# State-space tiles: panel splits issued later, gate Silu once per group, skip factor on ScalarE, last group in pieces, stick-breaking mask on GpSimd

## What is computed

```python
def _ssd_chunked(xs, dt, a_neg, bm, cm):        # 4 groups x 8 heads x 64, chunks of 128 tokens
    ...
    def step(state, inp):
        xc, ac, bc, cc = inp
        acum = jnp.cumsum(ac, axis=1)
        seg = jnp.where(causal, acum[:, :, None] - acum[:, None, :], -jnp.inf)
        scores = jnp.einsum('btgn,bsgn->btsg', cc, bc)[..., None] * jnp.exp(seg)
        y_diag = jnp.einsum('btsgh,bsghp->btghp', scores, xc)
        y_off = jnp.einsum('btgn,bghpn->btghp', cc, state) * jnp.exp(acum)[..., None]
        w_end = jnp.exp(acum[:, -1:] - acum)
        new_state = (state * jnp.exp(acum[:, -1])[..., None, None]
                     + jnp.einsum('bsgn,bsghp->bghpn', bc, xc * w_end[..., None]))
        return new_state, y_diag + y_off

# mixer: xbc = silu(conv4(h @ in_w)); after the scan
    y = y + d_skip.astype(jnp.float32)[:, None] * xs.astype(jnp.float32)
    y = y.reshape(b, s, M_D_INNER) * jax.nn.silu(z.astype(jnp.float32))
    yg = y.reshape(b, s, M_GROUPS, M_D_INNER // M_GROUPS)
    yg = yg * lax.rsqrt(jnp.mean(yg * yg, axis=-1, keepdims=True) + EPS)
    y = yg.reshape(b, s, M_D_INNER) * norm_g.astype(jnp.float32)
    return y.astype(h.dtype) @ out_w

# stick-breaking attention, per block of 128 queries
    mask = ((lo + jnp.arange(SB_BLOCK))[:, None] > jnp.arange(hi)[None, :])[None, None]
    log_keep = jnp.where(mask, jax.nn.log_sigmoid(-z), 0.0)
    after = lax.cumsum(log_keep, axis=3, reverse=True) - log_keep
    log_a = jnp.where(mask, jax.nn.log_sigmoid(z) + after, -jnp.inf)
```

## Time and profile before

| | |
|---|---|
| Runs, median (lowest to highest) | 3469.09 us (3468.8 to 3474.67) |
| The profiled execution, own time | 3467.17 us |
| Its span, first to last instruction | 3465.5 us |
| TensorE busy | 3122.3 us (90%) |
| VectorE, ScalarE, GpSimd busy | 1830.7, 1020.5, 421.3 us |
| Mean granted TensorE clock | 0.946 of full speed |

### The profile page before, as it was taken

How to read it: one execution, slowest core, us unless ns; L and a number is a source line. 1 busy time by engine, 2 the same in 40 slices (tenths; PEclk the granted TensorE clock), 3 DMA queues, 4 the chain that set the end, 5 groups by cost and what they waited for, 6 DMA issues and landing times.

```text
span 3465.5 us, 40303 instructions
## 1 busy us (share of the span) xinstructions
PE 3122.3 (90%) x16613; PEld 2420.0 (70%) x16613; DVE 1830.7 (53%) x1822; ACT 1020.5 (29%) x1252; POOL 421.3 (12%) x368
## 2 busy tenths in 40 slices
PE   4988799999979999999978999999966997999987
PEld 3765456666768888888756786878755885666666
DVE  6444683454244454443366756657554226776752
ACT  3111424454121111111123424333232113444432
POOL 0001000000131111110131302021124003000001
PEclk8988899999979999999979999999978999999998
DMA  5333000000114333331113324232310221112201
GB/s 207 109 98 98 28 1 1 1 1 7 43 37 122 109 102 110 121 97 49 38 31 89 104 66 117 67 110 85 91 61 19 85 91 61 43 49 62 74 19 61
DMA packets 241698, 239.28 MB, mean 69 GB/s; under 512 B 11701, under 2 KB 207122, under 8 KB 241554
## 3 DMA queue, kind: packets, MB, share of 16 engines
q1 hardware_dynamic: 219024, 163.34, 15.7%
q0 software_dynamic: 16080, 54.30, 5.0%
q10 hardware_dynamic: 6450, 19.57, 1.6%
HBM read 210.83 MB, written 26.35 MB: 68 GB/s over the span
## 4 chain that ended last, share of the span: by engine, by line
PE 75%; DVE 14%; ACT 5%; issue 3%; POOL 2%; DMA 1%; ACTq 0%; DVEq 0%; POOLq 0%
PE PU L830 14%; PE PU L831 14%; PE PU L832 14%; PE PU L1123 3%; DVE n_h L2131 2%; PE PU L1079 2%; PE PM L1430 2%; PE PM L1418 2%; PE PM L1145 2%; PE PM L1132 2%; PE PU L1407 2%; PE PM L1450 1%; PE PU L844 1%; PE PM L1452 1%; PE PM L1451 1%
## 5 line engine op out<-in xcount | busy, mean ns | idle before, releaser
L830 PE MATMUL PU<-hH,w_hi_t 128*128 128x512 f32 (+1 forms) x1920 | 769.0, 401 | 37.8 <-DVE w_lo_t L2052 31.5
L831 PE MATMUL PU<-hL,w_hi_t 128*128 128x512 f32 (+1 forms) x1920 | 755.4, 393 | 0.0
L832 PE MATMUL PU<-hH,w_lo_t 128*128 128x512 f32 (+1 forms) x1920 | 755.3, 393 | 0.0
L830 PEld LDWEIGHTS PU<-hH,w_hi_t 128*128 128x128 f32 (+1 forms) x1920 | 364.7, 190 | 120.5 <-DVE w_lo_t L2052 34.2
L2052 DVE TENSOR_TENSOR w_lo_t<-w_raw,w_hi_t 128x1024 fp32r<-128x1024 f32 x189 | 244.6, 1295 | 355.3 <-ACT w_hi_t L1508 315.6
L832 PEld LDWEIGHTS PU<-hH,w_lo_t 128*128 128x128 f32 (+1 forms) x1920 | 364.1, 190 | 79.9
L831 PEld LDWEIGHTS PU<-hL,w_hi_t 128*128 128x128 f32 (+1 forms) x1920 | 365.0, 190 | 77.5 <-issue 2.2
L1508 ACT ACTIVATE w_hi_t<-w_raw 128x1024 fp32r<-128x1024 f32 x173 | 180.8, 1045 | 535.2 <-PE PU L832 417.8
L2450 DVE SCALAR_TENSOR_TENSOR xT<-PU,mod,xT 128x1024 f32<-128x1024 f32 x120 | 154.0, 1283 | 207.9 <-PE PU L832 207.9
L844 PE MATMUL PU<-hH,w_hi_t 128*128 128x512 f32 (+1 forms) x272 | 117.2, 431 | 88.2 <-DVE hL L2116 87.8
L2708 DVE TENSOR_TENSOR_SCAN s_keep<-s_keep,zero 128x256 f32<-128x256 f32 (+7 forms) x128 | 184.5, 1442 | 1.8 <-ACT s_keep L1957 1.8
(11 more groups left out here) (358 smaller groups left out, 5171.9 us busy)
## 6 DMA issues: line engine op xcount, KB each, us to landing
ada_w<-in_ada_w_dram POOLq DMA_DIRECT2D x64, 384.0 KB, 4.1
w_raw<-in_w_gu_dram SPq DMA_DIRECT2D x44, 512.0 KB, 3.8
w_raw<-in_m_in_w_dram SPq DMA_DIRECT2D x40, 512.0 KB, 4.1
ada_w<-in_w_ada_dram POOLq DMA_DIRECT2D x32, 512.0 KB, 4.6
seg<-decay_sums SPq DMA_DIRECT2D x32, 512.0 KB, 4.6
w_raw<-in_w_down_dram SPq DMA_DIRECT2D x22, 512.0 KB, 3.6
w_raw<-in_w_in_dram SPq DMA_DIRECT2D x17, 512.0 KB, 3.8
ada_w<-in_w_ada_dram SPq DMA_DIRECT2D x16, 512.0 KB, 18.1
```

The source lines that it names most:

```text
L830: mm(PU[0:width, up, half, :], whi, aH[:, k, cols], start=k == 0, stop=False)
L831: mm(PU[0:width, up, half, :], whi, aL[:, k, cols], start=False, stop=False)
L832: last = mm(PU[0:width, up, half, :], wlo, aH[:, k, cols], start=False, stop=k == kt - 1)
```

## The change

- **Splits**: in the tile part the `split()` of an even tile moves behind `decays` on ScalarE and between `segments` and `masked` on VectorE.
- **Gate**: in groups 0 to 2 the four z units are evacuated with Copy, and after tile 7 ScalarE applies Silu to all four (`z_act`), ahead of the next group's first `split()`. Group 3 keeps Silu at each odd tile.
- **Skip factor**: the GpSimd multiply L769 goes. ScalarE scales the x tile in place, after `token_major`, before the store to `scr_x`. The factor's load and copy move to an earlier place.
- **Group 0**: on VectorE `step_sizes_2` runs before `conv(0, 0)`, and splits run ahead of `step_sizes_3`, `step_sizes_4` and `decay_tables`. On TensorE the scores of tile 0 move into the middle of the first z unit, those of tile 1 behind it.
- **Group 3's end**: tiles 0 to 6 are gated before `output(3, 7)`, tile 7 after it; TensorE sums each of the four squared tiles (32 matmuls for 8) and the GpSimd additions go; scale and low halves alternate, and the first projection unit waits for one tile at a time.
- **Stick-breaking mask**: the two bf16 matmuls of a step go. GpSimd sets the masked part of the last 128 columns of `s_keep` to 1 (two `affine_select` of 128x128 fp32 a step), between ScalarE's sigmoid and VectorE's scan, which now waits for it (`s_mk`). The GpSimd gate multiplies follow at fixed steps.
- Two semaphores of the rotary tables become one.

```diff
@@ -764,10 +761,8 @@
                         g.wait_ge(ss_y, TT * i + c)
                     nc.gpsimd.tensor_tensor(xdt[:, :].rearrange("p (h d) -> p h d", h=8), x3, heads(dt_t, i, c),
                                             ALU.mult).then_inc(ss_x, 1)
-                    g.wait_ge(el_landed[c % 2], 48 * (4 * i + c // 2 + 1))
-                    skip = xl[:, c % 2, :, :]
-                    nc.gpsimd.tensor_tensor(skip, skip, d_col[:, i, :].unsqueeze(2).broadcast_to([P, 4, P]),
-                                            ALU.mult).then_inc(ss_x, 1)
+                if i == NG - 1:
+                    break
                 sq = [xt[:, :, f * P:(f + 1) * P] for f in range(4)]
                 for dst, src, ready in ((sq[0], sq[1], 2), (sq[2], sq[3], 4)):
                     g.wait_ge(m_sq, 4 * i + ready)
...
-                                    base=0, pattern=[[-1, P]], channel_multiplier=1).then_inc(s_mk, 1)
+            link(nc.gpsimd.memset(zero[:, :], 0.0))
             nc.gpsimd.memset(s_keep[:, :, T:T + 1], 1.0).then_inc(s_mk, 1)
-            for n in range(2 * (SB_PAIRS - 1)):
+
+            def next_gate(n):
+
                 g.wait_ge(z_s, n + 1)
                 z = s_z[:, (n // 2 + 1) % 2, n % 2 * 512:(n % 2 + 1) * 512]
                 nc.gpsimd.tensor_tensor(z, z, z_sig[:, :], ALU.mult).then_inc(z_m, 1)
+
+            for s in range(SB_STEPS):
+                for n in (2 * s, 2 * s + 1):
+                    g.wait_ge(s_sg, n + 1)
+                    last = s_keep[:, n % 3, T - P:T]
+                    nc.gpsimd.affine_select(out=last, in_=last, compare_op=ALU.is_gt, fill=1.0, base=0,
+                                            pattern=[[-1, P]], channel_multiplier=1).then_inc(s_mk, 1)
+                if s % TT in (6, 7) and s < SB_STEPS - TT:
+                    next_gate(2 * (s // TT) + s % TT - 6)
             add_squares()
 
 
...
@@ -1316,9 +1318,16 @@
                 last.then_inc(ss_y, 1)
 
             def group_sums(i):
-                pe.wait_ge(m_add, 3 * (i + 1))
-                for t in range(TT):
-                    last = mm(PM[:, 2, t:t + 1], xt[:, t, 0:P], ones[:, 0:1], start=True, stop=True)
+
+                tiles = 1 if i < NG - 1 else 4
+                for f in range(tiles):
+                    if i < NG - 1:
+                        pe.wait_ge(m_add, 3 * (i + 1))
+                    else:
+                        pe.wait_ge(m_sq, 4 * i + f + 1)
+                    for t in range(TT):
+                        last = mm(PM[:, 2, t:t + 1], xt[:, t, f * P:(f + 1) * P], ones[:, 0:1],
+                                  start=f == 0 and t == 0, stop=f == tiles - 1 and t == TT - 1)
                 last.then_inc(n_sum, 1)
 
...
@@ -1353,14 +1362,18 @@
                 if i:
                     group_out(i - 1)
                 for f in range(4):
-                    ssd_scores(i, 2 * f)
+                    late = i == f == 0
+                    if not late:
+                        ssd_scores(i, 2 * f)
 
                     def mid():
                         if f:
                             ssd_out(i, 2 * f - 1)
-                        ssd_scores(i, 2 * f + 1)
+                        ssd_scores(i, 2 * f + (0 if late else 1))
 
                     feat_unit(panel_ready(), 0, P, KD, hH, hL, mid=mid)
+                    if late:
+                        ssd_scores(i, 1)
                     ssd_out(i, 2 * f)
             ssd_out(NG - 1, TT - 1)
...
                     for hd in range(2):
                         r = slice(hd * HD, (hd + 1) * HD)
-                        mm(PU[:, hd, half, 0:w - half * 512], s_q[r, b, qt * P:(qt + 1) * P],
-                           s_k[r, b, half * 512:w], start=True, stop=half < qt // 4)
-                for hd in range(2):
-                    mm(PU[:, hd, qt // 4, (qt % 4) * P:(qt % 4 + 1) * P], eye[:, :], upper[:, :],
-                       start=False, stop=True).then_inc(s_s, 1)
+                        ins = mm(PU[:, hd, half, 0:w - half * 512], s_q[r, b, qt * P:(qt + 1) * P],
+                                 s_k[r, b, half * 512:w], start=True, stop=True)
...
@@ -1847,14 +1858,15 @@
                 act.wait_ge(unit_free[n % 2], n // 2 + 1)
                 dst = c_acc[:, j % 2, :] if j < 4 else (bT if j == 4 else cT)[:, :]
                 af(dst, c_acc[:, j % 2, :], ACT.Silu).then_inc(cv_act, 1)
-                if j < 4:
-                    act.wait_ge(cv_act, 6 * i + j + 1)
-                    act.dma_start(scr_x[i, j, :, :], c_acc[:, j % 2, :]).then_inc(x_stored[j % 2], 16)
 
             def token_major(i, j):
                 act.wait_ge(cv_tr, 5 * i + j + 1)
                 dst = bt[:, :, :] if j == 4 else xt[:, :, j * P:(j + 1) * P]
                 af(dst, stat_ps.rearrange("p (t c) -> p t c", c=P), ACT.Copy).then_inc(cv_tok, 1)
+                if j < 4:
+                    rows = c_acc[:, j % 2, :]
+                    link(af(rows, rows, ACT.Copy, scale=d_col[:, i, j:j + 1]))
+                    act.dma_start(scr_x[i, j, :, :], rows).then_inc(x_stored[j % 2], 16)
 
             def group_squares(i):
                 for f in range(4):
...
@@ -1900,15 +1912,21 @@
                         passed(2)
                         if c == 0:
                             activate(i, 5)
+                last = i == NG - 1
                 for c in range(TT):
-                    if c % 2 == 0:
-                        split()
                     if c == 0 and i == 0:
                         activate(i, 5)
                     decays(i, c)
-                    if c % 2:
+                    if c % 2 == 0:
+                        split()
+                    else:
                         p = unit()
-                        free(af(zf[:, c // 2, :], unit_ps(p), ACT.Silu))
+                        free(af(zf[:, c // 2, :], unit_ps(p), ACT.Silu if last else ACT.Copy))
+                if not last:
+                    zp, zn = uc.at(-1)
+                    act.wait_ge(unit_free[zp], zn + 1)
+                    for f in range(4):
+                        af(zf[:, f, :], zf[:, f, :], ACT.Silu).then_inc(z_act, 1)
             group_squares(NG - 1)
...
-                ve.wait_ge(ss_x, (3 * TT - 1) * i + (3 * c + 3 if c < TT - 1 else 3 * TT - 1))
+                ve.wait_ge(ss_x, (2 * TT - 1) * i + (2 * c + 2 if c < TT - 1 else 2 * TT - 1))
+                ve.wait_ge(el_landed[b], 48 * (4 * i + c // 2 + 1))
                 diag = PM[:, 0, :]
                 if c:
-                    ve.wait_ge(el_landed[b], 48 * (4 * i + c // 2 + 1))
                     link(V.tensor_tensor(y, PM[:, 1, :], ea[:, b, :, :].rearrange("p f t -> p (f t)"), ALU.mult))
                     link(V.tensor_tensor(y, y, diag, ALU.add))
...
+                ve.wait_ge(ss_g, TT * (NG - 1) + end)
+                for f in range(4):
+                    n = m_unit(NG - 1) + 6 + KD + f
+                    ve.wait_ge(unit_free[n % 2], n // 2 + 1)
+                    z3 = zf[:, f, first * P:end * P].rearrange("p (t c) -> p t c", c=P)
+                    ins = V.tensor_tensor(z3, z3, xt[:, first:end, f * P:(f + 1) * P], ALU.mult)
+                    if signal:
+                        ins.then_inc(m_gate, 1)
...
@@ -2622,20 +2649,20 @@
             for i in range(NG):
                 if i == 0:
                     split()
+                    step_sizes_2()
                     conv(0, 0)
-                    step_sizes_2()
                     split()
                     conv(0, 1)
+                    split()
                     step_sizes_3()
+                    conv(0, 2)
                     split()
-                    conv(0, 2)
                     step_sizes_4()
-                    split()
                     conv(0, 3)
                     split()
                     conv(0, 4)
+                    split()
                     decay_tables()
-                    split()
                     conv(0, 5)
                 else:
                     split()
...
@@ -2658,21 +2685,26 @@
                     for c in range(4):
                         down_units("m_g", (2 * c, 2 * c + 1))
                 for c in range(TT):
-                    if c % 2 == 0:
-                        split()
-                        skip()
                     if c >= 2:
                         state_update(i, c - 2)
                         output(i, c - 2)
                     segments(i, c)
+                    if c % 2 == 0:
+                        split()
+                        skip()
                     masked(i, c)
                 state_update(i, TT - 2)
             output(NG - 1, TT - 2)
+            last_gated(0, TT - 1, False)
             output(NG - 1, TT - 1)
-            gated(NG - 1)
+            last_gated(TT - 1, TT, True)
             group_inverse(NG - 1)
-            group_scale(NG - 1)
-            group_low(NG - 1)
+            group_scale(NG - 1, (0, 1))
+            group_low(NG - 1, (0,))
```

(6 more changed lines are left out.)

54 lines of the change are left out of this document (23 added, 31 removed).

## The result

| | before | changed |
|---|---|---|
| Median (lowest to highest), same chip | 3469.01 us (3468.8 to 3474.67) | 3438.44 us (3436.73 to 3442.19) |
| Profiled execution, own time | 3467.17 us | 3439.78 us |
| Its span, TensorE busy, mean granted clock | 3465.5 us, 90%, 0.946 | 3438.2 us, 91%, 0.944 |

The ratio is 0.9909 (95% interval 0.9892 to 0.9927): 0.9% faster. The forecast was 3449 us, between 3432 and 3464. A second measurement of the changed kernel, on another chip, gave 3441.62 us, ratio 0.9922 (0.9909 to 0.9936).

A forecast was written before the change was run, and what follows sets the result against it. VectorE's loop was taken to bound the tile part, with TensorE 90% busy overall. Terms of -1, -7.4, -3.4, -5, +0.8, -3.5 and -0.4 summed to -19.9 us from 3467.17; with 1.9 for the median, 3449 us, range 3432 to 3464.

The forecast's parts named there:

- Stick-breaking: Mask moved to GpSimd: 5.6 us of matmuls saved, against 3.5 and 1.7 us of collisions; -0.4 us (-6 to +8).
- main case: Whole kernel: the forecast itself comes true, with a time of 3440 to 3457 us; chance 0.58.
- sign of being wrong: Whole kernel: the forecast is wrong if the group-end wait is absent, the time then being under 3440 us.
- Group 0's convolutions: Both 5.8 us waits for `w_lo_t` go, and some low-clock time: -7.4 us, bounds -5.8 and -8.3.
- The group's end: `output(6)` queues behind a split awaiting ScalarE: TensorE waits 6.7 us, and the low clock costs 2 to 2.6 more.
- Tiles of groups 0 to 2: Tile loop: pairs get 2.5 us shorter, mostly given back at the group's end; -1 us (-9 to +4).
- An even tile becomes 8.0 + 2.1 = 10.1 us: VectorE's loop, groups 0 to 2: without table loads, with the split behind; a pair 18.1 us, 2.5 less.
- Group 3's tiles: Silu and its loads stay; a pair takes 19.4 against some 21.9 us: -5 us (-8 to 0).
- Scores of tile 0: Group 0: half a unit fills the wait for C's Silu, 4.5 us remain, 3 more in `ssd_out(0)`; -3.4 us (-5 to 0).
- Sums and projection: After group 3: four slow sums replace the GpSimd wait, +0.8 us; the projection starts earlier, -3.5 us (-5 to -2).
- GpSimd's mask bounds: Stick-breaking: from 0.95 us held per select VectorE bounds all pairs; 3466 to 3470 or 3503 us; chance 0.08.
- the tile gain stays: Groups 0 to 2: Silus miss the path at the group's end, up to 10 us gained each; 3425 to 3437, chance 0.18.

The follow-up runs named there:

- e3: Changed kernel with VectorE's work in group 0 (step sizes, decay tables) put back behind the convolutions, ahead of the splits: 3449.69 us.
- e1: Changed kernel with one exchange on VectorE: at the head of groups 1 to 3 the output of tile 6 comes before the split: 3419.84 us.
- e10: Changed kernel with both tile-loop edits undone: split ahead of the tile's work, gate's Silu at every second tile: 3439.29 us.
- e5: Changed kernel with the split put back ahead of the tile's work in every even tile, Silu still once a group: 3428.76 us.
- e13: e11 with group 3 treated like the others: split ahead of the tile's work, four Silus behind the group: 3394.15 us.
- e6: Changed kernel with the scores of tile 0 in group 0 ahead of the first gate unit again: 3440.89 us.
- e4: Changed kernel with the gate's Silu back at every second tile in all groups, split left behind: 3434.77 us.
- e11: Changed kernel with split ahead of tile work in groups 0 to 2, tile 6's output before the split, group 3's squares added on VectorE: 3400.52 us.

## Why the prediction was right, and where it was not

The sign and the range held, and most terms came out near their size; the sum was 20 us for a measured 27 to 31. Stick-breaking is the largest part of what was missed (3.7 us in the trace, some 5 by the means), then groups 1 and 2 (2.1); 2.3 us lie ahead of the mixer, where nothing was forecast and executions differ by 5. The first median, 3438.4 us, lies under the 3440 to 3457 in which the prediction put its main case, and under the 3440 that it tied to a missing wait at the group's end. That wait was there; the second median is 3441.6. So that sign of being wrong was set too close.

- **Group 0's convolutions**, -7.4: right. 7.9 us by both traces, and 7.9 back in e3.
- **The group's end**, wait 6.7 us and low clock: right, 5.8 us and the clock as said; e1 confirms queue order as the cause and the price, 8 us a group. The part behind L1309 of tile 7 grew by 1.9 and 2.8 us in groups 2 and 1, for the 2 to 2.6 forecast. What the prediction didn't ask is how cheaply the wait goes away.
- **Tiles of groups 0 to 2**, -1: it was -3.7 in groups 1 and 2 alone, for -1.6, and the walk behind it held. It had TensorE reach the last L1307 10.1 us earlier (2146.7 for 2158.81 - 2.05), less 2.5 for collisions; measured are 82.2 - 74.4 = 7.8 us, and then the wait gives most of it back. The collisions were right too: 18 of VectorE's tile instructions in groups 0 to 2, six a group, run over their usual 1.23 or 0.69 us before, by 14.2 us in all; in the changed kernel 8 do, by 6.7 (2.2 us a group). The skip factor alone, e10, leaves 13, by 9.4, and is 5.1 us faster than before in three groups, 1.7 a group, the "two of six collisions". What the prediction lacks is a price for each edit alone. "An even tile becomes 8.0 + 2.1 = 10.1 us" is true for both together, but was never set against the Silu made once with the split left where it was, 9.2 to 9.8. When I did price that, for e5, I wrote 8.0 + 2.1 + 1.2 = 11.3 us, and this step failed: the 2.1 us of idle time are the load's and the Silu's, and go with them.
- **Group 3's tiles**, -5: 4.2 and 5.0 us in the two traces of the changed kernel. Of these the skip factor has 1.9 to 2.7 (83.1 to 81.2 us in e5 and 80.4 in e10, which have the same group 3) and the moved split some 2: the Silu stays in each pair there, so the split behind the work is a gain, of some 0.7 us a pair where 1.2 was said. And here the better answer was the other one, by e13: 6.8 us more.
- **Scores of tile 0**, -3.4: mis-sized. The stretch to the third score came 2.6 us shorter, but e6 prices the edit itself at 0.9 us there and at nothing by the fourth. The remaining wait of 4.4 us was right. The second wait was put at 3 us; it is 4.0, and brings the low clock, 0.9 us.
- **Sums and projection**, +0.8 and -3.5: +0.1 and -3.0. One sum takes 3.5 us at the lower clock, as read from the row before.
- **Stick-breaking**, -0.4: mis-sized, about -5. The matmuls' 5.6 us were right. The 5.2 us against them were mine: I let scans pay for selects, from a row in which a scan came second. The failed term is the 0.25 us that a select was to hold VectorE up; measured are 0.7 us more of waits for `s_w` at the ends of the pairs and 0.6 in the last pair. The Trainium skill, page "SBUF — State Buffer", section "Who interferes with whom", says more than I took from it: it is the order of issue, and not the kind of operation, that decides which of the two blocks. The trace agrees: the selects, short and mostly second (114 of 128), reach 1.78 us, and the scans stay at 1.49 (640 columns). I had priced the scans and given the selects a sentence. The rival "GpSimd's mask bounds" had no part in it, though its alarm did sound: the median select holds 0.85 us, and 63 of the 128 hold over the 0.9 us at which the prediction saw 3460 us coming.
- **The rival "the tile gain stays"** needed the wait at the group's end to be absent. It wasn't, and the time stayed above that rival's 3437 us; e1 is the rival carried out, at 3420 us.

## What to carry to other kernels

Two edits that aim at the same idle row are not to be added: write the loop's length for each alone and for both, since the second may sit on the wrong side once the first is in. Where a critical step stands behind a step that nobody awaits on the same queue, look for the exchange of the two before you count the wait as given back. A wait that an engine spends idle can be cheaper than narrow work that fills it.

## What the hardware showed that was not expected

- A GpSimd select of 128x128 beside VectorE's work took 0.29 to 1.78 us, and VectorE's scans of 640 columns stayed at 1.49 us. All 114 selects that began during a VectorE instruction ended 0.09 to 0.20 us after it. The first to start runs at its own pace, and the other one pays: a gate multiply (1.27 us) that came first made the 768-wide scan 2.81 us long before the change.
- Thirteen microseconds of 128x1 matmuls without a gap ran at a granted clock of 0.50 to their end. TensorE was "busy" for all of it, and the clock did not rise.
- A TensorE wait of 5.1 to 5.8 us was always followed by matmuls at 0.50; waits of 2.04 us in e4 were not (L1308 took 1.16 us). Waits of that length and shorter ones go either way: behind 2.02 and 2.04 us in e10 L1308 took 1.32 and 1.66 us; and there a wait of 1.73 us was followed by L1308 at 1.16 us (at 2102.78) and another of the same length, in the same group, by 2.08 us (at 2124.96).
- From scores to scores a group repeats to 0.1 us when TensorE sets the pace (185.2 to 185.6 us in e11 and e13), and varies when VectorE does: 195.5 to 200.6 us for the same groups in the changed kernel, its repeat and e3, whose tile loops are the same.
